# Two weight chunks by k-tile, value products beside the next scores, and two tensors at other addresses

## Time and profile before

| | us |
|---|---|
| median of three runs | 417.97 |
| the profiled execution's own time | 418.06 |
| span in its trace | 416.2 |
| PE busy | 406.7 (98%) |
| DVE busy | 334.3 (80%) |
| ACT busy | 250.2 (60%) |

### The profile page before, as it was taken

How to read it: one execution, slowest core, us unless ns; L and a number is a source line. 1 busy time by engine, 2 the same in 40 slices (tenths; PEclk the granted TensorE clock), 3 DMA queues, 4 the chain that set the end, 5 groups by cost and what they waited for, 6 DMA issues and landing times.

```text
span 416.2 us, 7060 instructions
## 1 busy us (share of the span) xinstructions
PE 406.7 (98%) x2839; PEld 374.2 (90%) x2839; DVE 334.3 (80%) x444; ACT 250.2 (60%) x298; POOL 28.5 (7%) x40
## 2 busy tenths in 40 slices
PE   8999999999999999999999999999999999999993
PEld 7999988999999999889998898999999999999982
DVE  5588566967757437874958888999999999999976
ACT  7664328763665534551556648777777777777743
POOL 0069300000000000000200000000000000000003
PEclk9999999999999999999999999999999999999997
DMA  8999655443235255555453245556555555555002
GB/s 288 420 419 393 205 195 183 150 139 138 102 111 193 102 203 202 186 183 172 168 171 134 101 145 192 187 209 204 205 202 201 200 200 204 198 207 228 2 0 101
DMA packets 12539, 77.47 MB, mean 186 GB/s; under 512 B 1376, under 2 KB 1376, under 8 KB 4064
## 3 DMA queue, kind: packets, MB, share of 16 engines
q1 hardware_dynamic: 12512, 77.09, 51.3%
HBM read 76.04 MB, written 1.05 MB: 185 GB/s over the span
## 4 chain that ended last, share of the span: by engine, by line
PE 93%; DVE 2%; ACT 1%; DMA 1%; issue 1%; SPq 0%; POOL 0%; POOLq 0%; DVEq 0%; ACTq 0%
PE bank L1119 42%; PE bank L1385 16%; PE bank L1138 16%; PE bank L1233 11%; PE bank L1245 1%; DVE res L1054 1%; DMA head_all<-in_head_dram 1%; PE bank L1331 1%; PE bank L1351 1%; PE bank L1152 1%; PE bank L1274 1%; PE bank L1265 0%; PE bank L1344 0%; PE bank L1195 0%; PE bank L1209 0%
## 5 line engine op out<-in xcount | busy, mean ns | idle before, releaser
L684 DVE TENSOR_TENSOR w_lo<-raw,w_hi 128x2048 fp32r<-128x2048 f32 (+2 forms) x87 | 148.4, 1715 | 25.7 <-ACT w_hi L439 24.0
L1119 PE MATMUL bank<-hT_hi,w_hi 128*128 128x256 f32 x416 | 117.1, 281 | 1.0 <-DVE w_lo L684 0.6
L1119 PE MATMUL bank<-hT_lo,w_hi 128*128 128x256 f32 x416 | 116.1, 279 | 0.0
L1119 PE MATMUL bank<-hT_hi,w_lo 128*128 128x256 f32 x416 | 116.0, 279 | 0.0
L1119 PEld LDWEIGHTS bank<-hT_hi,w_hi 128*128 128x128 f32 x416 | 78.2, 188 | 2.4 <-DVE hT_lo L738 1.0
L1119 PEld LDWEIGHTS bank<-hT_hi,w_lo 128*128 128x128 f32 x416 | 79.1, 190 | 0.0
L1119 PEld LDWEIGHTS bank<-hT_lo,w_hi 128*128 128x128 f32 x416 | 78.3, 188 | 0.6
L439 ACT ACTIVATE w_hi<-raw 128x2048 fp32r<-128x2048 f32 x33 | 62.9, 1915 | 26.3 <-PE bank L1119 12.6
L684 DVE TENSOR_TENSOR t_lo<-t_sum,t_hi 128x1024 fp32r<-128x1024 f32 x30 | 36.8, 1228 | 0.0
L1233 PE MATMUL bank<-hT_hi,w_hi 128*128 128x256 f32 x128 | 36.5, 285 | 0.0
L1233 PE MATMUL bank<-hT_lo,w_hi 128*128 128x256 f32 x128 | 35.6, 278 | 0.0
(11 more groups left out here) (196 smaller groups left out, 822.7 us busy)
## 6 DMA issues: line engine op xcount, KB each, us to landing
raw<-in_weights_dram SPq DMA_DIRECT2D x65, 1024.0 KB, 4.9
head_all<-in_head_dram SPq DMA_DIRECT2D x7, 256.0 KB, 4.4
raw<-in_chunk_dram SPq DMA_DIRECT2D x4, 256.0 KB, 5.5
raw<-in_chunk_dram SPq DMA_DIRECT2D x2, 512.0 KB, 6.7
res<-in_x_dram SPq DMA_DIRECT2D x2, 512.0 KB, 11.5
mem_tok<-in_mem_dram SPq DMA_DIRECT2D x1, 1024.0 KB, 12.8
memT_raw<-in_memT_dram SPq DMA_DIRECT2D x1, 1024.0 KB, 11.3
out_dram<-xs SPq DMA_DIRECT2D x2, 512.0 KB, 2.7
```

The costliest lines, as they stand in the source:

```text
L684: return nc.vector.tensor_tensor(dst, whole, high.bitcast(fp32), sub)
L1119: last = mm(outs[m], w, v[:, k0 + k, :], start=first and n == 0, stop=k == nk - 1 and n == 2, skip_group_check=bool(kt_wait))
```

## The change

- Head: the transfers are now x and chunk 0 of k-tiles 0 and 1 (two pieces), both k-tiles of chunk 1 in one piece (`pair`), and then six triples of x, chunk 0 and chunk 1 for k-tiles 2 to 7. PE takes the products of both chunks tile by tile and within a step by kind: all high by high, then those with hT_lo, then those with w_lo, each kind with its own wait. Both chunks count as used at the end of the last triple.
- Pair loop: PE goes gate 2p, sums, first half of gate 2p+1, transposes, attended values of pair p-1, scores of pair p+1, second half of gate 2p+1; the attended values of pair 3 stand by themselves behind the loop. `sb_aT` alternates between three buffers. The second bank of the transposes is bank 0 instead of 3, and the row of the memory's rstd goes through bank 7 behind the sums of pair 0 instead of bank 1 ahead of gate 0. ACT and DVE follow this order.
- Places: mT and aT stand at 320 and 64, as hT does. No other tensor moves by this.

```diff
-        mT_hi_all, _ = by_tokens("mT_hi", 0, 192)
+        mT_hi_all, _ = by_tokens("mT_hi", 0, 320)
-        mT_lo_all, _ = by_tokens("mT_lo", 0, 320)
+        mT_lo_all, _ = by_tokens("mT_lo", 0, 64)
...
+        sb_aT1 = sb("sb_aT1", [P, 2, 384], over=o + 12288)
...
-        aT_hi_all, _ = by_tokens("aT_hi", 0, 192)
+        aT_hi_all, _ = by_tokens("aT_hi", 0, 320)
-        aT_lo_all, _ = by_tokens("aT_lo", 0, 320)
+        aT_lo_all, _ = by_tokens("aT_lo", 0, 64)
...
-        MO_S, MO_PT, SB_Z, ATT_O = (2, 3), (6, 3), (4, 5), 7
+        MO_S, MO_PT, SB_Z, ATT_O = (2, 3), (6, 0), (4, 5), 7
-        X_ROW_BANK, MEM_ROW_BANK = 7, 1
+        X_ROW_BANK, MEM_ROW_BANK = 7, 7
...
+            for j in range(HEAD_PIECES):
+                dst = piece(j) if j else head_all[:, HEAD - 2 * SEQ:HEAD + GAINS]
+                sp.dma_start(dst, (head0, head1, pair)[j] if j <= PAIR else triples[j - PAIR - 1])\
+                    .then_inc(head_arrived[j], 16)
+            for i, (k0, k1) in enumerate(CHUNK2):
+                sp.dma_start(raw[:, 2, k0 * SEQ:k1 * SEQ], chunk2[i]).then_inc(half_in[i], 16)
...
+            def head_high(k):
+                act.wait_ge(head_arrived[piece_of(k)], 16)
+                copy(hT_hi[:, k, :], x_in_head(k), ACT.Copy, scale=gT[:, G_MIX + k:G_MIX + k + 1])\
+                    .then_inc(hi_done[X], 1)
+                ready, n = (piece_hi, 1) if k < KT - 1 else (w_hi_ready, 2)
+                copy(w_tile(w_hi, k), w_in_head(k), ACT.Copy).then_inc(ready, n)
...
-                if p:
-                    act.wait_ge(sb_av, p)
-                copy(sb_aT[:, :, :], banks[:, SB_Z[0]:SB_Z[1] + 1, 0:384], ACT.Exp).then_inc(sb_exp, 1)
-                split(GATE0 + 2 * p + 4)
+                if p == 1:
+                    act.wait_ge(sumsq_dve, 2)
+                if p == 2:
+                    act.wait_ge(sb_av, 1)
+                copy(sb_weights(p)[:, :, :], banks[:, SB_Z[0]:SB_Z[1] + 1, 0:384], ACT.Exp).then_inc(sb_exp, 1)
+                split(GATE0 + 2 * p + 4)
+                if p:
+                    att_high(p - 1)
                 if p + 1 < HEADS // 2:
                     softplus_exp(p + 1)
-                att_high(p)
                 split(GATE0 + 2 * p + 5)
+            att_high(HEADS // 2 - 1)
...
-            spread(mem_row, MEM_ROW_BANK, 2)
...
                 gate_out(2 * p)
+                if p == 0:
+                    spread(mem_row, MEM_ROW_BANK, 2)
+                if p + 1 < HEADS // 2:
+                    split(GATE0 + 2 * p + 4)
                 dve.wait_ge(mo_t, p + 1)
                 if p:
                     dve.wait_ge(sb_av, p)
                 for i in range(2):
                     last = nc.vector.tensor_copy(mo_pT[:, i, :], bank[MO_PT[i]][:, 0:384])
                 last.then_inc(mo_pt, 1)
-                split(GATE0 + 2 * p + 4)
+                if p:
+                    att_low(p - 1)
                 if p + 1 < HEADS // 2:
                     scores(p + 1)
                 gate_out(2 * p + 1)
-                att_low(p)
...
+                x_tiles = 1 + max(k for _, k in tiles)
+                pe.wait_ge(hi_done[X], x_tiles)
+                pe.wait_ge(*((w_hi_ready, 2) if last else (piece_hi, n)))
+                products(w_hi, hT_hi)
+                pe.wait_ge(lo_done[X], x_tiles)
+                products(w_hi, hT_lo)
+                pe.wait_ge(*((w_lo_ready, 2) if last else (piece_lo, n)))
+                products(w_lo, hT_hi)
+            for k in range(FIRST):
+                head_products([(0, k)], k + 1)
+            head_products([(1, k) for k in range(2)], PAIR + 1)
+            for k in range(FIRST, KT):
+                head_products([(0, k), (1, k)], piece_of(k) + 1, last=k == KT - 1)
...
+            def attend(p):
+                pe.wait_ge(mo_pt, p + 1)
+                pe.wait_ge(*((att_lo, p) if p else (row_ready, 2)))
+                attended(p)
             for p in range(HEADS // 2):
+                if p:
+                    pe.wait_ge(mo_pt, p)
...
-                pe.wait_ge(mo_normed, p + 1)
                 if p == 0:
                     pe.wait_ge(v_evac, 4)
+                    spread_rstd(MEM_ROW_BANK, 2)
+                else:
+                    pe.wait_ge(gate_evac, 2 * p)
+                pe.wait_ge(w_lo_ready, GATE0 + 2 * p + 2)
+                gate(2 * p + 1, 0)
+                pe.wait_ge(mo_normed, p + 1)
+                pe.wait_ge(gate_evac, 2 * p + 1)
                 for i in range(2):
                     for j in range(3):
                         t = tr(bank[MO_PT[i]][:, P * j:P * j + P], mo_u[:, i, P * j:P * j + P], ident[:, :])
                 t.then_inc(mo_t, 1)
-                pe.wait_ge(*((gate_evac, 2 * p) if p else (row_ready, 2)))
-                pe.wait_ge(w_lo_ready, GATE0 + 2 * p + 2)
-                gate(2 * p + 1, 0)
+                if p:
+                    attend(p - 1)
                 if p + 1 < HEADS // 2:
                     scores(p + 1)
                 gate(2 * p + 1, 1).then_inc(w_used, 1)
-                pe.wait_ge(mo_pt, p + 1)
-                if p:
-                    pe.wait_ge(att_lo, p)
-                attended(p)
+            attend(HEADS // 2 - 1)
```

More of the change, by code:

```diff
@@ L55, in weight_chunks, with hybrid_layer @@
     return cols, at
-def hybrid_layer(nc, x, head0, head, chunk1, chunk2, mem, memT, g_final, weights, ff, out):
+def hybrid_layer(nc, x, head0, head1, pair, triples, chunk2, mem, memT, g_final, weights, ff, out):
     fp32, f32r = mybir.dt.float32, mybir.dt.float32r
@@ L110, in hybrid_layer, with piece_of @@
     GAINS = 32
-    PIECES = [(0, k, k + 1) for k in range(KT)] + [(1, k, k + 2) for k in range(0, 8, 2)] + [(2, 0, 4), (2, 4, 8)]
-    def piece_no(i):
-        return sum(k1 < KT for _, _, k1 in PIECES[:i + 1])
+    FIRST, PAIR, HEAD_PIECES = 2, 2, KT + 1
+    CHUNK2 = [(0, 4), (4, 8)]
+    def piece_of(k):
+        return k if k < FIRST else k + 1
     ctx = ExitStack()
@@ L262, in hybrid_layer @@
         raw_in = [sem(f"raw_in{s}") for s in range(RAW)]
-        head_arrived = [sem(f"head_arrived{k}") for k in range(KT - 1)] + [raw_in[0]]
-        piece_in = [sem(f"piece_in{i}") for i in range(len(PIECES))]
+        head_arrived = [sem(f"head_arrived{j}") for j in range(HEAD_PIECES - 2)] + [raw_in[1], raw_in[0]]
+        half_in = [sem("half_of_chunk2_in"), raw_in[2]]
         piece_hi, piece_lo = sem("piece_hi"), sem("piece_lo")
@@ L452, in high_in @@
                     .then_inc(hi_done[n], 1)
[L454 to L463, removed]
-                    .then_inc(hi_done[X], 1)
[L465 to L468, removed]
+            def head_high(k):
+                act.wait_ge(head_arrived[piece_of(k)], 16)
+                copy(hT_hi[:, k, :], x_in_head(k), ACT.Copy, scale=gT[:, G_MIX + k:G_MIX + k + 1])\
+                    .then_inc(hi_done[X], 1)
+                ready, n = (piece_hi, 1) if k < KT - 1 else (w_hi_ready, 2)
+                copy(w_tile(w_hi, k), w_in_head(k), ACT.Copy).then_inc(ready, n)
+            for k in range(FIRST):
+                head_high(k)
+            act.wait_ge(head_arrived[PAIR], 16)
+            copy(w_hi[:, 1, 0:2 * SEQ], piece(PAIR), ACT.Copy).then_inc(piece_hi, 1)
+            for k in range(FIRST, KT):
+                head_high(k)
+            for i, (k0, k1) in enumerate(CHUNK2):
+                cols = slice(k0 * SEQ, k1 * SEQ)
+                act.wait_ge(half_in[i], 16)
+                copy(w_hi[:, 2, cols], raw[:, 2, cols], ACT.Copy).then_inc((piece_hi, w_hi_ready)[i], 1)
             split(3)
@@ L734, in _ @@
             nc.vector.memset(zeros[:, :], 0.0).then_inc(zeros_ready, 1)
[L735 to L745, removed]
+            for k in range(FIRST):
+                head_low(k)
+            dve.wait_ge(piece_hi, PAIR + 1)
+            low(w_lo[:, 1, 0:2 * SEQ], piece(PAIR), w_hi[:, 1, 0:2 * SEQ]).then_inc(piece_lo, 1)
+            for k in range(FIRST, KT):
+                head_low(k)
+            for i, (k0, k1) in enumerate(CHUNK2):
+                cols = slice(k0 * SEQ, k1 * SEQ)
+                dve.wait_ge(*((piece_hi, HEAD_PIECES), (w_hi_ready, 3))[i])
+                low(w_lo[:, 2, cols], raw[:, 2, cols], w_hi[:, 2, cols]).then_inc((piece_lo, w_lo_ready)[i], 1)
             split(3)
@@ L827, in _ @@
                 gate_out(2 * p + 1)
-                att_low(p)
+                if p + 1 == HEADS // 2:
+                    split(GATE0 + 2 * p + 4)
+                    att_low(p)
                 split(GATE0 + 2 * p + 5)
@@ L1160, in _, with head_products, products, chunk2_halves @@
                 mm(bank[7][:, 0:P], zeros[:, :], zeros[:, :], start=True, stop=True)
[L1163 to L1166, removed]
-                    for i, (chunk, k0, k1) in enumerate(PIECES):
-                        if (chunk, k0) == (c, k):
-                            pe.wait_ge(*((w_lo_ready, c + 1) if k1 == KT else (piece_lo, piece_no(i))))
-                return wait
```

(24 more changed lines are left out.)

54 lines of the change are left out of this document (29 added, 25 removed).

## The result

The changed kernel took 415.76 us (median of 7 runs, 415.03 to 416.79), the kernel before beside it on the same chip 418.15 (7 runs, 417.77 to 419.56). The ratio is 0.9932, with a 95% interval of 0.9918 to 0.9947: 2.2 to 3.4 us faster. The forecast was 416.0 (415.0 to 417.3). In a later job the same kernel had 415.67 and 0.9923. Between jobs the kernel before moved by about 1 us (medians of 418.8 to 419.3 in the four later ones), so runs of different jobs are compared by their ratios.

The account below looks back on a forecast made before the run. PE's in-order product stream, 98% busy, was taken as the bound. Head 0.2, pair loop 0.9 and places 0.9 sum to 2.0 us off 418.06, 416.06, and 0.09 lower for the median: 416.0 (range 415.0 to 417.3).

Parts of the forecast that it names:

- the joints: Pair loop: fewer changes to and from plain float32 products, all three kinds costed alike, save 0.65 us (0.3 to 0.84).
- What bounds the kernel now: Whole kernel: PE's in-order product stream, 98% busy, sets the end; savings up to about 240 us come off it.
- what would show it: Signs: chunk 3 starting at 22.3 to 22.6, pairs of 16.0 to 16.1 us, branches 5.44 to 5.5, later stages unchanged.
- Part 1, the head: Chunks 0 and 1 tile by tile: 0.2 us gained; most of 0.8 becomes a longer wait ahead of chunk 3.
- Rival B: Head: fewer small transfers bring chunk 3 earlier by 0.6 us or more, total 415.5; chance 0.1.
- Part 2, the pair loop: New order of the pair loop: 0.9 us gained, 0.65 from fewer joints and 0.25 from a stall removed.
- the row's stall: Pair 0: gate 1 no longer waits for the copy of the memory's row, 0.25 us gained.
- The covers: Pair loop: ACT and DVE stay ahead of PE, no queue within 1 us, 1.8 us of slack left for sp_lo.
- rival C: Pair loop: the stick-breaking chain becomes the bound, with a wait for sp_lo ahead of L1263, total 418.8; chance 0.06.
- D: Pair loop: joints don't shrink inside the joined block, leaving the loop 0.25 us alone, total 416.65; chance 0.14.
- Part 3, the places: mT and aT moved: memory-chunk, branch and weight-moving products run faster, 0.9 us gained (0.3 to 1.6).
- Rival A: Memory chunks and branches: the new place of mT and aT gives nothing, total 416.9; chance 0.2.

Follow-up runs that it names:

- e4_no_head: Changed kernel with the head of before, so new pair loop and new places alone: 416.70 us, ratio 0.9942.
- e3: Kernel before with the new head and its DMAs alone: 418.77 us, ratio 0.9991.
- e6: Changed kernel with one extra 64-column product ahead of each MLP up-chunk from the third on: 417.54 us, ratio 0.9959.
- e7: Changed kernel with attended(2) moved ahead of the first half of gate 7, no longer behind the transposes: 417.24 us, ratio 0.9959.
- e11: Changed kernel with an extra 128-column product of hT_hi by itself ahead of chunk 4: 415.61 us, ratio 0.9925.
- e12_after_again: The changed kernel once more, unaltered, in a later job: 415.67 us, ratio 0.9923.
- e9: Changed kernel with the head of before and an extra 128-column product of neg_tri_r by itself ahead of chunk 4: 415.85 us, ratio 0.9922.
- e1_place: Kernel before with mT and aT moved to 320 and 64 and nothing else: 418.96 us, ratio 0.9999.
- e5: Changed kernel with one extra 128-column product ahead of each MLP up-chunk from the third on: 417.52 us, ratio 0.9966.
- e10: Changed kernel with 128-column products of neg_tri_r ahead of chunk 4 and of hT_hi and w_hi between the first two triples: 415.45 us, ratio 0.9912.
- e8: Changed kernel with an extra 128-column product of neg_tri_r by itself ahead of chunk 4: 415.60 us, ratio 0.9927.
- e2: Kernel before with the new order of the pair loop alone: 417.56 us, ratio 0.9968.

## Why the prediction was right

**The total: right, in part by luck.** Gain forecast 2.0 us, measured 2.39 by the medians. The loop and the places give 1.14 and 1.31 in the rows, and e4_no_head, which has just these two, was timed at 2.4. The terms behind the sum are right less often than the sum: too little for the joints was made up by a pace that I had not seen, and 0.9 for the places was a choice between 0.3 and 1.6.

**"What bounds the kernel now": right.** The gain lies in the product stream ahead of the MLP; the steps of the MLP behind 256 us are unchanged (5.65 for 48, 4.76 for 21), as "what would show it" asked.

**Part 1, the head: a term mis-sized.** The step that failed is that PE is done with chunk 2 at 21.7 and that "nearly all of the 0.8 us turns into a longer wait ahead of chunk 3", leaving 0.2. In the nine profiles with the new head PE was free for chunk 3 between 21.57 and 23.13. Five have no wait there (after, e3, e6, e7, e11), and the longest is 0.22 us, in e12_after_again. There the chain goes over chunk 3's split, as forecast; the second fence is PE's timeline, where the next product was due at 22.08:

```profile
6.50 11.47 DMA raw<-in_weights_dram
...
18.00 1.93 ACT w_hi L455
...
19.95 2.30 DVE w_lo L707
...
22.30 3.01 PE bank L1152 x24
```

```profile
21.97 0.28 PE L1152 MATMUL bank<-hT_hi,w_lo 128*128 128x256 f32 x1
22.30 0.39 PE L1152 MATMUL bank<-hT_hi,w_hi 128*128 128x256 f32 x1
```

Two things made PE late that the sum had at nothing. The triples and chunk 2 went at 113.3 ns, as counted, in three profiles only (e7, e11, e12); in the other six they went at 117.8, which is 0.54 us over the last 120 products. And the third piece arrived at 6.46 in the profile shown, where before's third came at about 4.9. Neither is the change's doing alone: e4 and e9 ran their old heads slow, and the third piece was also late in e1_place and e9_no_head_kick (6.12 and 5.90), and in by 5.07 in e7_parity with the new head. My baseline was a good draw. Against the average of the old head the part is worth some 0.4 us, which no timing sets apart from nothing. What sets the pace of the triples is open. PE stood idle ahead of the third piece or of the first triple in after, e3, e5, e6 and e10 (0.21 to 0.89 us), and all five went slow; without such a wait e7, e11 and e12 went fast and e8 slow. With the old head before, e1 and e2 went fast behind waits of 0.27 to 0.66 us, e4 and e9 slow behind waits of 0.28 and 0.57.

Rival B is not settled by this. Its first condition (chunk 3 landing 0.6 earlier) was met in the two profiles compared, 17.58 for 18.32, and its sign (chunk 3 starting before 22.1) in three of nine, 21.57, 21.94 and 22.09. Its mechanism was not: the two stretches of the earlier trace rows moved 359 and 421 GB/s now, no more than before. ACT began chunk 3's copy anywhere from 16.93 to 18.65 with the new head (mean 17.87) and from 17.32 to 18.71 with the old one (mean 18.26), so on average it landed 0.4 us earlier, within that spread.

**Part 2, the pair loop: the sum near, the terms not.** 0.9 forecast, 1.14 measured; pairs of 16.14 and 16.12 us where 16.0 to 16.1 stood. Equal pace is had by pair 1: 16.33 before, 16.12 now, so a joined pair saves 0.2. Slow gate products were 144 before (two runs in pair 0, one long one each in pairs 2 and 3) and are 24 now: 120 x 4.5 ns = 0.54. With the 0.25 of the row's stall, which went as forecast, 0.35 is left for the joints, where I had 0.65, near my lower bound of 0.3. The step that failed is to "count the same" for transposes and scores as for the attended values. The gate products of pair 1 took 5.64 and 2.75 us in the earlier trace rows, 8.39 in sum, and take 8.18 in one row now, because no run is entered from attended values: that way in costs 0.20, and the ways in from transposes (5.46 for 48) and scores (2.75 for 24) 0.02 to 0.03. Before there were four entries from attended values, now there are two, which makes 0.40. What I had not seen is the pace, though the 5.64 and 5.85 stood in the earlier trace rows. Inside the joined block the change from transposes to attended values and on to scores is free: 1.45 us for the 16 products, as before. The covers held; PE has no wait on DVE in the loop, so rival C is out, and by the 0.35 D too.

**Part 3, the places: the size right, the mechanism half.** 0.9 forecast; measured 28.46 - 27.40 = 1.06 for the 240, -0.04 for the 48 of the second memory chunk (5.62 to 5.66), and 0.23 for the weights moved by mT and aT (5.57 to 5.50, 11.16 to 11.00): 1.25 in sum. "Which one a run of products falls into seems to be settled at its start" was right, and e7_parity, one profile, shows by what in this place: the pace of the run ahead, turned over by the attended values. I weighed it as chance, "of the three pairs entered from these two were slow", and could have read the rule off those rows. The gate ahead of the 240 was fast before, so with the old order the new places had to give nothing, and e1_place says so. Rival A was right of the places alone and wrong of the change.

The Trainium skill's TensorE: Matmul & The Clock Gate, in the section on step-by-step phases, says that the weight load has a read port of its own and takes nothing from the running product. The prediction read this as: where the operands lie does not matter; the page itself says nothing of places. e2_loop and e4_no_head differ in the place alone, enter the 240 from the same rows, and take 28.47 and 27.40: the measurement decides against that reading.

## What to carry to other kernels

When one long stream of like products is the bound, divide every row of the chain by its count: two paces 4% apart at one granted clock are worth more than the joints between stages. Test parts of a change in the combination too, since a place and an order gave 1.06 us together in a row where each alone gave nothing. And before a stage is costed from one execution, ask how that stage falls in others: the shown head of before was 0.5 us better than its mean.

## What the runs showed of the hardware

- Runs of f32r products with 256 columns went at 113.3 or at 117.8 ns with the granted clock at 1.00 in both stretches compared, moved weights of 512 columns at 229 or 233. In the runs read, the pace was there within the first five products and was carried over chunks and changes of bank; in 10 of 10 profiles without an extra product at that place chunk 4 went on at the pace of chunk 3's second half.
- With mT and aT at 64 and 192 bytes from the weights' place only the slow pace was seen (28.46 or 28.47 in before, e2, e3); at 192 and 448 either (28.46 in e1 and e7, 27.40 in the other nine).
- Behind attended values, plain float32 products of 128*64 tiles, the pace was the opposite of that of the run before them, in all of before, after, e1, e3, e4 and e7. In e2 the 240, at the old place, stayed at the slow pace behind 24 at the slow pace (3.02). Behind the MLP's down products the pace was always slow.
- A 128-column product of neg_tri_r by itself turned slow into fast (e8, e9) and left fast alone (e10, 2.74 for the 24 ahead and 21.81 for the 192); of hT_hi, or of hT_hi and w_hi, it left slow alone (e11, e10), and so did one of ident_r and neg_tri_r in the MLP (e5). Each is one profile. Why a place in a partition matters to TensorE is open, and so is what sets the pace behind the row product in chunk 3: fast in before, e1, e7 and e10, slow in the other ten.
